# FFN up/gate product of a two-layer decoder trunk: one 512-column matmul for x_hi and x_lo, and an add of the two halves on VectorE

## What is computed

```python
def conv_ffn(x, w_in, conv_w, conv_b, w_out):
    up, gate = jnp.split(x @ w_in, 2, axis=-1)
    up = lax.conv_general_dilated(up, conv_w[:, None, :], window_strides=(1,),
        padding=[(CONV_WIDTH - 1, 0)], dimension_numbers=("NWC", "WIO", "NWC"),
        feature_group_count=up.shape[-1]) + conv_b
    return (jax.nn.gelu(up) * gate) @ w_out
...
        f = conv_ffn(x, ffn_w_in[layer], ffn_conv_w[layer], ffn_conv_b[layer], ffn_w_out[layer])
        x = layer_norm(DEEPNORM_ALPHA * x + f, ln_g[layer, 1], ln_b[layer, 1])
```

## Time and profile before

| | |
|---|---|
| median of 3 runs | 651.89 us (650.15 to 653.15) |
| span of the profiled execution | 650.9 us |
| TensorE busy | 634.1 us, 97%, 3901 matmuls |
| VectorE busy | 408.3 us, 63% |
| ScalarE busy | 337.9 us, 52% |
| mean granted TensorE clock | 0.993 |
| chain that ended last | 92% TensorE, 3% VectorE, 2% ScalarE |

### The profile page before, as it was taken

One profiled execution on the slowest core, in us unless ns is written; L12 is line 12 of the kernel. 1 busy time (PEld: TensorE's weight loads), 2 busy tenths in 40 slices (PEclk: granted clock), 3 DMA queues, 4 the chain that ended last, 5 costly groups with the idle time before them and its releaser, 6 DMA issues.

```text
span 650.9 us, 10509 instructions
## 1 busy us (share of the span) xinstructions
PE 634.1 (97%) x3901; PEld 549.4 (84%) x3901; DVE 408.3 (63%) x728; ACT 337.9 (52%) x550; POOL 63.8 (10%) x85
## 2 busy tenths in 40 slices
PE   8999999999999999999979999999999999999995
PEld 6776776789999999999868787787999999999994
DVE  5765475487655566556685665867765565665566
ACT  5676556357444444444335785774554444444440
POOL 5400000330000000000340010026000000000002
PEclk9999999999999999999989999999999999999999
DMA  8972353145555555555347624423655555555511
GB/s 291 337 274 83 108 174 107 66 135 189 194 193 193 193 186 171 169 185 191 130 140 269 237 66 156 168 70 126 197 192 191 175 174 176 186 174 175 176 56 65
DMA packets 68682, 109.68 MB, mean 168 GB/s; under 512 B 2044, under 2 KB 47404, under 8 KB 68140
## 3 DMA queue, kind: packets, MB, share of 16 engines
q1 hardware_dynamic: 68012, 105.09, 48.0%
q0 software_dynamic: 640, 4.20, 1.6%
HBM read 108.23 MB, written 1.05 MB: 168 GB/s over the span
## 4 chain that ended last, share of the span: by engine, by line
PE 92%; DVE 3%; ACT 2%; DMA 1%; issue 1%; SPq 0%; DVEq 0%; ACTq 0%
PE wide L1052 17%; PE wide L1053 16%; PE wide L1054 15%; PE score L1052 6%; PE score L1054 6%; PE score L1053 6%; PE outb L1053 3%; PE outb L1052 3%; PE turn L1054 3%; PE turn L1053 3%; PE turn L1052 3%; PE outb L1054 3%; PE turn L1144 1%; PE score L1136 1%; PE score L1135 1%; DMA raw<-in_a_w_qkv 1%
## 5 line engine op out<-in xcount | busy, mean ns | idle before, releaser
L781 DVE TENSOR_TENSOR w_lo<-raw,w_hi 128x2048 fp32r<-128x2048 f32 (+1 forms) x115 | 205.8, 1807 | 107.2 <-ACT w_hi L579 107.2
L579 ACT ACTIVATE w_hi<-raw 128x2048 fp32r<-128x2048 f32 (+1 forms) x125 | 183.8, 1496 | 67.3 <-PE wide L1054 41.9
L1052 PE MATMUL wide<-w_hi,xT_hi 128*128 128x512 f32 (+1 forms) x256 | 99.7, 389 | 2.3 <-DVE w_lo L839 1.5
L1054 PE MATMUL wide<-w_hi,xT_lo 128*128 128x512 f32 (+1 forms) x256 | 94.3, 368 | 0.0
L1053 PE MATMUL wide<-w_lo,xT_hi 128*128 128x512 f32 (+1 forms) x256 | 93.9, 367 | 0.0
L1052 PE MATMUL score<-xT_hi,w_hi 128*128 128x256 f32 x320 | 90.6, 283 | 0.0
L1054 PE MATMUL score<-xT_hi,w_lo 128*128 128x256 f32 x320 | 90.5, 283 | 0.0
L1053 PE MATMUL score<-xT_lo,w_hi 128*128 128x256 f32 x320 | 90.4, 283 | 0.0
L1053 PE MATMUL wide<-w_lo,hT_hi 128*128 128x512 f32 x176 | 70.5, 400 | 0.0
L1052 PE MATMUL wide<-w_hi,hT_hi 128*128 128x512 f32 x176 | 69.6, 396 | 0.0
L1054 PE MATMUL wide<-w_hi,hT_lo 128*128 128x512 f32 x176 | 69.2, 393 | 0.0
(11 more groups left out here) (164 smaller groups left out, 1135.8 us busy)
## 6 DMA issues: line engine op xcount, KB each, us to landing
raw<-in_ffn_w_in SPq DMA_DIRECT2D x44, 1024.0 KB, 5.1
raw<-in_ffn_w_out SPq DMA_DIRECT2D x22, 1024.0 KB, 4.8
raw<-in_a_w_qkv SPq DMA_DIRECT2D x9, 1024.0 KB, 8.2
raw<-in_w_kv_shared SPq DMA_DIRECT2D x8, 1024.0 KB, 5.1
raw<-in_a_w_o SPq DMA_DIRECT2D x4, 1024.0 KB, 4.8
raw<-in_b_w_q SPq DMA_DIRECT2D x4, 1024.0 KB, 5.1
raw<-in_b_w_o SPq DMA_DIRECT2D x4, 1024.0 KB, 4.8
raw<-in_a_w_qkv SPq DMA_DIRECT2D x6, 512.0 KB, 8.9
```

The costliest lines, as they stand in the source:

```text
L579: ins = nc.scalar.activation(w_hi[slot][:, part], raw[slot][:, part], ACT.Copy)
L781: ins = nc.vector.tensor_tensor(w_lo[slot][:, part], raw[slot][:, part], w_hi[slot][:, part].bitcast(F32), ALU.subtract)
L1052: nc.tensor.matmul(dst, a_hi, b_hi, start=start, stop=False, skip_group_check=True)
L1054: return nc.tensor.matmul(dst, a_lo, b_hi, start=False, stop=stop, skip_group_check=True)
```

## The change

The two x tiles become one, `xT`, with a leading index for hi and lo. In `features`, for each k tile, one matmul with `w_hi` stationary streams x_hi and x_lo together, 512 columns, into the whole bank: the left half collects w_hi*x_hi, the right half w_hi*x_lo. A second matmul with `w_lo` stationary streams x_hi, 256 columns, and adds into the right half. VectorE then adds the two halves of each bank into SBUF (`up_sum`, `gate_sum`) with a `tensor_reduce` that reads the bank with the two halves as the innermost dimension. The tap and convolution read `up_sum`, and `hidden` reads `gate_sum`. The banks are released by the sums.

```diff
     def up_of(first, tt):
-        return wide[2 + tt][:, 0:SEQ] if first else up_bank[tt][:, 0:SEQ]
+        return wide[2 + tt][:, 0:SEQ] if first else up_sum[:, tt, :]
     def gate_of(first, tt):
-        return wide[2 + tt][:, SEQ:2 * SEQ] if first else gate_bank[tt][:, 0:SEQ]
+        return wide[2 + tt][:, SEQ:2 * SEQ] if first else gate_sum[:, tt, :]
...
-        xT_hi = sb("xT_hi", [P, KT, SEQ], F32R)
-        xT_lo = sb("xT_lo", [P, KT, SEQ], F32R)
+        xT = sb("xT", [P, 2, KT, SEQ], F32R)
+        xT_hi, xT_lo = xT[:, 0, :, :], xT[:, 1, :, :]
...
+        up_sum = sb("up_sum", [P, 2, SEQ])
+        gate_sum = sb("gate_sum", [P, 2, SEQ])
...  (ScalarE, ffn_group)
-                        elif tt == 0:
-                            act.wait_ge(up0_done, t - layer)
                         else:
-                            act.wait_ge(chunk_used, cu + 1)
+                            act.wait_ge(up_summed, 2 * (t - layer) - 1 + tt)
...  (VectorE, ffn_group)
+                    def add_parts(tt, total, bank, ready, summed):
+                        dve.wait_ge(*ready[tt])
+                        nc.vector.tensor_reduce(total[:, tt, :], bank[tt][:, :].rearrange("p (a q) -> p q a", a=2),
+                                                AX.X, ALU.add).then_inc(summed, 1)
                     for tt in range(2):
                         up = up_of(first, tt)
+                        if not first:
+                            add_parts(tt, up_sum, up_bank, ((up0_done, t - layer), (chunk_used, cu + 1)), up_summed)
                         dve.wait_ge(tap_done, 2 * t + tt + 1)
...
-                        elif tt == 0:
-                            dve.wait_ge(gate0_done, t - layer)
                         else:
-                            dve.wait_ge(chunk_used, cg + 1)
+                            dve.wait_ge(gate_summed, 2 * (t - layer) - 1 + tt)
...
                         split_after(cu, slot_u)
+                    for tt in range(2):
+                        if not first:
+                            add_parts(tt, gate_sum, gate_bank, ((gate0_done, t - layer), (chunk_used, cg + 1)),
+                                      gate_summed)
                     for tt in range(2):
                         make_hidden(tt)
...  (TensorE, features)
+                        parts = banks[tt][:, :].rearrange("p (a q) -> p a q", a=2)
                         for kt in range(KT):
                             cols = slice(kt * 2 * P + tt * P, kt * 2 * P + (tt + 1) * P)
-                            last = product(banks[tt][:, 0:SEQ], w_hi[slot][:, cols], w_lo[slot][:, cols],
-                                           xT_hi[:, kt, :], xT_lo[:, kt, :], kt == 0, kt == KT - 1)
+                            nc.tensor.matmul(parts, w_hi[slot][:, cols], xT[:, :, kt, :], start=kt == 0, stop=False,
+                                             skip_group_check=True)
+                            last = nc.tensor.matmul(parts[:, 1, :], w_lo[slot][:, cols], xT_hi[:, kt, :], start=False,
+                                                    stop=kt == KT - 1, skip_group_check=True)
...
-                             None if second else [(conv_done, 2 * t - 1), (conv_done, 2 * t)], up0_done,
+                             None if second else [(up_summed, 2 * (t - layer) - 3 + tt) for tt in range(2)], up0_done,
...
-                             None if second else [(hidden_done, 2 * t - 1), (hidden_done, 2 * t)], gate0_done)
+                             None if second else [(gate_summed, 2 * (t - layer) - 3 + tt) for tt in range(2)], gate0_done)
```

More of the change, by code:

```diff
@@ L389, in yoco_trunk @@
         hhi_done, hlo_done = sem("hhi_done"), sem("hlo_done")
+        up_summed, gate_summed = sem("up_summed"), sem("gate_summed")
         block = ctx.enter_context(nc.Block())
```

## The result

The changed kernel takes 657.53 us in the median (655.88 to 659.07, 4 runs) against 651.69 us (650.15 to 653.15) before, a ratio of 1.0098 with a 95% interval of 1.0074 to 1.0121: 5.8 us, about 1%, slower. The forecast was 652.0 us with a range to 657. The profiled execution has a span of 657.3 us, 6.4 above that of before, and a mean granted clock of 0.985.

A forecast was written before the change was run, and what follows sets the result against it. The prediction took TensorE's matmul starts to bound the feed-forward. From a span of 650.9 us, -4.0 for fewer starts and +4.0 for group 10's stalls left 650.9; the median forecast was 652.0 us, range 647 to 657.

The forecast's parts named there:

- What bounds the kernel; the place of the loss: Feed-forward groups: the distance between TensorE's matmul starts counts; a wait opens at group 10, where the cover is gone.
- What TensorE gains: Feed-forward k tiles: one start fewer of three saves 6.3 ns each, 4.0 us in all; bounds 0 and 8.1.
- rows 3: Earlier trace of a loop group: 512-column matmuls 0.2333 us apart, pricing the new pair at 0.3531 us.
- rows 4: Earlier trace of the projections: 512-column matmuls 0.2270 us apart, pricing the pair at 0.3468 us, 8.1 us in all.
- What VectorE pays: Four reduces a group on VectorE, each 0.69 us, 0.61 from start to start; upper bound 1.22.
- A loop group: VectorE's chain in the loop: second convolution pair 2.06 us later, loop still TensorE's with 0.4 us a group to spare.
- hop to ScalarE 0.03: Loop group: the time from the end of VectorE's sum to the start of ScalarE's tap, taken as 0.03 us.
- rival 4: Loop: VectorE becomes the bound, from 0.1 us more per reduce; some 658 us, or 682 at the upper bound; chance 0.11.
- The delay is worked off at 0.4 a group: Loop: VectorE's late start in group 1 brings no stall and is gone by group 5, at 0.4 us a group.
- It stalls for 1.9, with the hop 2.0 us, in each layer: Group 10: TensorE waits for hT_lo, 2.0 us in each layer, 4.0 us in all.
- Rival 2: Group 10: the stall brings TensorE's clock down in both layers, +3.4 us, 655.4 us, slower; chance 0.14.
- The sum: Whole kernel: 4.0 us gained and 4.0 us of stalls cancel, 652.0 us, no change; chance 0.43.

The follow-up runs named there:

- e1: The change with TensorE's 512- and 256-column matmuls but no sums, left half of each bank read straight: 645.46 us against 651.32 before.
- e8: The change with the tap's scale and bias columns fixed in loop groups, so no register instruction stands between wait and tap: 653.31 us against 651.44 before.
- e2: The change with its 512-column matmul cut into two of 256 columns, sums, waits and banks kept: 658.56 us against 651.32 before.
- e3: The change with both up sums put ahead of the first convolution step on VectorE: 647.72 us against 651.32 before.
- e6: The change for the up banks alone, gate made and read as before: 650.12 us against 651.60 before.
- e5: The change for the gate banks alone, up made and read as before: 650.16 us against 651.60 before.
- e7: e3 with the first gate sum also moved, ahead of the up chunk's w_lo: 646.99 us against 651.60 before.
- e4: The change with 14 matmuls of zeros on TensorE where it stalls for group 10's hT_lo: 654.45 us against 651.32 before.

## Why the prediction was wrong

**What bounds the kernel; the place of the loss: right.** TensorE's matmul starts set the feed-forward, and the cover that was missing was at group 10.

**"What TensorE gains" (4.0 us): low.** e1 shows 5.9. The bounds 0 and 8.1 hold it. The pair costs between the 0.3531 that I took from rows 3 and the 0.3468 from rows 4, one in some groups and the other in the rest. I treated the two prices as rivals; both occur in one loop.

**"What VectorE pays" (0.69 us a reduce): right,** 0.68 to 0.69 measured, no more than the tensor_tensor of the earlier trace rows takes for 512 numbers in a row. The upper bound of 1.22 did not come. The note on PSUM's lines in the Trainium skill (SBUF — State Buffer, "Door 1: The DMA port swizzle") speaks of matmuls; this VectorE read at a stride of 1 KB shows no slowing of that kind.

**"A loop group", with "hop to ScalarE 0.03": the step that failed.** The 0.03 was read between a convolution step and a gelu, whose operands hold no register. The tap's do, and its hop is 0.18 us in layer 0 and 0.24 in layer 1; without the register instruction it is 0.04 (e8). With the tap at 0.60 instead of 0.56 and the hop back at 0.15 to 0.17, a round trip is 1.62 and 1.70 us and not 1.43, twice a group. VectorE's chain is then 16.5 + 0.4 = 16.9 us in layer 0, where 16.80 are measured, and 16.5 + 0.5 = 17.0 in layer 1, where it is 16.97. TensorE's mean period is 16.80, so the 0.4 us "to spare" were not there. I had called this the narrow place and put it at risk only through a slower reduce (rival 4: "from 0.1 us more per reduce"); the 0.4 came from the hops instead.

**"The delay is worked off at 0.4 a group": fell with it.** In layer 0 VectorE reaches group 2 6.59 us behind TensorE's start instead of 5.04, 1.55 late, and is 1.44 late at group 10, since its period equals TensorE's. In layer 1 it starts 1.0 late and ends 1.8 late, as its period is the longer one.

**"It stalls for 1.9, with the hop 2.0 us, in each layer": near for its chain, wrong for the kernel.** e2, in which VectorE comes on time, has 1.9 us, with two misses of 0.15 to 0.2 us cancelling. The change has 3.7: the lateness of 1.4 is on top, and TensorE is 0.4 earlier within group 10.

**Rival 2 (chance 0.14) came true, and dearer than priced.** With a pause of 3.7 us the clock falls in the pause already and is low for 6.8 us, 5.3 of them behind it: 2.5 us a layer, not 1.7. At e2's pause of 1.9 it falls just behind the restart and is low for 3.4 us, which cost 1.6.

**The sum.** By the medians: -5.9 for TensorE (e1), and +11.7 for what the sums bring. The profiled spans of the change and of e1 are 11.4 us apart: two pauses (7.8), two slow stretches (5.0) and TensorE held in layer 1's loop (0.9), less 2.3 that e1's execution took longer before group 1 (0.8) and between the layers (1.5, with one stretch of low clock more). The prediction had -4.0 and +4.0, so the gain that it had too low hid 1.9 us of what it missed. Without the long hops (e8) the kernel takes 653.31, inside the range, and the sum closes: two pauses of 2.2 and two slow stretches of 1.6, less 5.9, is +1.7, with +1.9 measured. So by the medians the hops account for 4.2 of the 5.5 us by which the forecast was off. The rest is made up of the clock (3.2) and pauses 0.2 longer than forecast, less the 1.9 of gain. Its range to 657 left out just the mix that happened: a mild rival 4 feeding rival 2. I had added their chances as if they excluded each other, while here the short pauses at group 10 (0.75 and 0.87 us, e3 and e6) left the clock up, and all six of 1.9 us or more (e2, e8, the change) brought it down.

**Open.** What decides between 0.347 and 0.353 us for the pair was not tried. In e5 the gate's pair costs 0.354 throughout, in e6 the up pair 0.347. Nor was it tried why the hop differs between the layers, or what lets the clock stay up or fall between the layers.

## What to carry to other kernels

When a step is put ahead of a step on another engine, work out the round trip with the hop of that very instruction: whether the waiting instruction, or a register instruction ahead of it, carries the wait changed it here by 0.14 to 0.2 us. A chain as long as the busy engine's period keeps the delay that it starts with (the change, layer 0), one that is 0.3 us shorter works it off within the loop (e8); what is left is paid where the cover ends, behind the loop. Where an engine sends out two results and waits for an answer to each, let it send both first (e3), and fill the wait that is left with the next sum (e7).

## What the runs showed of the hardware

- A pause of TensorE of 0.75 or 0.87 us between dense products left the clock at its upper level (e3, e6). With pauses of 1.9 and 2.1 us it fell to 1.2 GHz within 0.7 us of the restart and stayed there for about 3.4 us (e2, e8); in the pauses of 3.7 us it fell 2.2 to 2.4 us after the last matmul and was low for 6.8 us (the change). 14 matmuls of zeros in the pause kept it up (e4). The pause of 1.8 us between the layers was followed by a low clock in some profiled executions and not in others (e4, e6).
- One 512-column and one 256-column matmul take 0.347 to 0.354 us from start to start, three of 256 columns 0.359; the one start less is worth 5 to 13 ns.
- A tensor_reduce over two halves of a bank, 512 numbers at a stride of 256, takes 0.68 to 0.69 us, the same as the tensor_tensor that reads 512 numbers in a row.
- From the end of a VectorE sum to the start of ScalarE's tap are 0.04 us where the tap carries the wait (written-out groups, e8), and 0.18 to 0.27 us where a register instruction ahead of it does (the loops of the change).
